# First norm of a hybrid encoder layer: TensorE turns x as it is loaded, the norm weights go on as a column behind the turn

## Chip, cores and metric

One core of a Trainium2 chip runs the whole layer as one program. The metric is device time in microseconds (us), median of the runs. Engines: PE is TensorE (PEld its weight loads), ACT is ScalarE, DVE is VectorE, POOL is GpSimd, SP is SyncE, which here only issues DMAs. 1 KB is 1024 bytes in the sizes of transfers.

## The reference, cut to what is computed

```
x = x + 1/2 * SwiGLU_1(RMSNorm(x, ffn1_norm))     # 2048 -> 2 x 5632 -> 2048
x = x + mix(RMSNorm(x, mix_norm))                 # dilated and differential attention, w_in, w_out
x = x + 1/2 * SwiGLU_2(RMSNorm(x, ffn2_norm))
rms_norm(x, g) = x * rsqrt(mean(x*x) + 1e-6) * g
swiglu_ffn(x) = (silu(gate) * up) @ w_out,  gate, up = split(rms_norm(x, g) @ w_in)
```

x is 256 rows of 2048 float32 values. Only the first norm, ahead of SwiGLU_1, is touched here.

## The kernel before

**Precision.** Every large product is made of three fp32r matmuls: an operand a is split into a_hi (rounded) and a_lo = a - a_hi, and hi·hi, hi·lo and lo·hi are added up in PSUM. So each piece of weights passes ACT (`split_hi`: w_hi is a rounded copy of w_raw) and then DVE (`split_lo`: w_lo = w_raw - w_hi) before TensorE may use it. Such a piece is a *unit*: two k-tiles of 128 by 512 columns, 128x1024 on chip, 12 matmuls of 512 columns. Units are numbered u0, u1, ... here. The ring of w_hi and w_lo has 4 places, so ACT may make unit u only when TensorE has used unit u-4. A weight load (`load`) brings 1024 KB, two units, into one of the 4 slots of w_raw. W0 is the load of u0 and u1, W1 that of u2 and u3, and so on; W4 is that of u8 and u9.

**The norm.** The factor rsqrt(...) of a row is applied later, to the product. What the matmuls need first is x·g, turned (transposed), in h_hi and h_lo. That is done in four chunks of 512 columns (four k-tiles each): SP loads a chunk of x and a chunk of the norm weights, the latter spread over all 128 partitions (`gain_row`); DVE multiplies them (`gain_x`, into `rows`); TensorE turns the product in 8 transposes (`turn_rows`, into `turn`); ACT copies it rounded to h_hi (`turn_split_hi`) and DVE subtracts to h_lo (`turn_split_lo`). Chunks 0 and 1 are turned before the first unit, chunk 2 between u0 and u1, chunk 3 between u3 and u4. The sum of squares of a row, for the factor, is made by ACT (`square_x`, two instructions for a chunk, each with an accumulator read).

**First stage of the FFN** (`hidden_first`): u0 to u7 make the first 512 columns of the gate, u8 to u15 those of the second half of w_in. u2 and u3 need chunk 1 of h, u4 and u5 chunk 2, u6 and u7 chunk 3. Each engine's order is written out by hand, and semaphores count units. Between the units DVE also makes the row factor (`norm_factor`, 14 tiny instructions in a chain, after `turn_split_lo` of chunk 3), `activation_wide` (after u9), `activation_sums` (after u10) and `split_sums` (after u11, waiting for ACT's s_hi), and only then w_lo of u12.

**The queue of SP** is one list: x and gain_row chunk by chunk with W0 to W2 between, then W3, then 17 small loads (rotary tables, head norm weights, lambda vectors; up to 64 KB each), then W4 on, each of these waiting for its slot.

The factor `splits` and the counters of `turn_hi` and `turn_split` number the turned chunks; `turn_rows(r, ...)` waits for `rows_ready` of r + 1.

Of the kernel before, what the change touches and what calls it, by code (L numbers as in the profile page):

```python
# [18 lines left out]
ALU = mybir.AluOpType  # L19
# [6 lines left out]
P = 128  # L26
# [93 lines left out]
IN1, OUT1, QKV, PROJ, IN2, OUT2 = range(6)  # L120
ROWS = np.cumsum([0, 4, FFN_ITERS, 4, 4, 4, FFN_ITERS]).tolist()
R_NORM1, R_FFN1, R_NORMX, R_MIX, R_NORM2, R_FFN2 = range(6)

# [30 lines left out]
def hybrid_layer_kernel(nc, x, ffn1_norm, ffn1_w_in, ffn1_w_out, mix_norm, w_in, a_q_norm, a_k_norm, b_q_norm,  # L156
# [8 lines left out]
    with ExitStack() as ctx:  # L165
# [24 lines left out]
        root = sb("root", [P, 88])  # L190
        gain_col = sb("gain_col", [P, 4])
        half_rstd = sb("half_rstd", [P, TT])

        with ExitStack() as hidden:
# [64 lines left out]

        x_landed = [sem(f"x_landed{c}") for c in range(4)]
        ident_landed = sem("ident_landed")
        const_landed = sem("const_landed")
        mask_landed = sem("mask_landed")
# [94 lines left out]
        def _(sp):  # L360
# [67 lines left out]

            gate_up1 = tiled(ffn1_w_in)  # L430
            for c in range(4):
                cols = slice(c * NC, (c + 1) * NC)
                sp.dma_start(x_sb[:, :, cols], x_dram[:, :, cols]).then_inc(x_landed[c], 16)
                sp.dma_start(gain_row[:, cols], ffn1_norm[:, cols].to_broadcast([P, NC])).then_inc(x_landed[c], 16)
                if c:
                    load(gate_up1, 0, KT * (c - 1), KT, c - 1)
            load(gate_up1, 0, KT * 3, KT, 3)
            sp.dma_start(cst[:, P:P + N_ROPE], consts[:, P + TT * SEQ:N_CONST]).then_inc(const_landed, 16)
            for gain, dst in ((a_q_norm, g_aq), (a_k_norm, g_ak), (a_out_norm, g_ao), (b_out_norm, g_bo),
                              (b_q_norm, g_bq), (b_k_norm, g_bk)):  # L440
# [12 lines left out]
            for g in range(GROUPS):  # L453
# [3 lines left out]
                if g == 0:  # L457
                    sp.wait_ge(units_used, UNIT[QKV])
                    sp.dma_start(mask[:, :, :], consts[:, P:P + TT * SEQ]
                                 .rearrange("p (t s) -> p t s", t=TT)).then_inc(mask_landed, 16)  # L460
            sp.wait_ge(rows_ready, ROWS[R_MIX])
            sp.dma_start(gain_row[:, :], ffn2_norm.to_broadcast([P, D])).then_inc(gain_landed, 16)
            proj_w = tiled(w_out)
            for n, (c, j) in enumerate(PROJ_ORDER):
# [10 lines left out]
        def _(pe):  # L475
# [27 lines left out]
            def turn_rows(r, buf, split, pair=None, copied=None):  # L503

                pair = buf if pair is None else pair
                pe.wait_ge(rows_ready, r + 1)
                if split is not None:
                    pe.wait_ge(turn_split, split)
                if copied is not None:
                    pe.wait_ge(turn_hi, copied)  # L510
                for k in range(4):
                    for t in range(TT):
                        mm = nc.tensor.transpose(turn4[pair][:, k, t * P:(t + 1) * P],  # L513
                                                 rows[:, buf, t, k * P:(k + 1) * P], ident)
                mm.then_inc(rows_turned, 1)

            h, act = (h_hi, h_lo), (act_hi, act_lo)

# [35 lines left out]
            def hidden_first(s_in, r0):  # L554

                u0 = UNIT[s_in]
                bank_wait(s_in, 0, 0)
                if s_in == IN1:
                    chunk(PARTS_D, u0, range(1), h, 0, r0 - 4)
                    turn_rows(r0 - 2, xg_at[2], splits(r0 - 3))  # L560
                    chunk(PARTS_D, u0, range(1, 4), h, 0, r0 - 4)
                else:
                    chunk(PARTS_D, u0, range(4), h, 0, r0 - 4)
                turn_rows(r0 - 1, 0, splits(r0 - 1))
                chunk(PARTS_D, u0, range(4, 8), h, 0, r0 - 4)
                bank_wait(s_in, 1, 0)
                chunk(PARTS_D, u0 + 8, range(8), h, 1)
# [171 lines left out]
            def attention_step(s):  # L739

                u, phase = divmod(s, 3)
                if phase == 0:
                    if u % HEADS_C == 2 and u > 2:
                        pe.wait_ge(turn_split, splits(ROWS[R_MIX] + u // HEADS_C))
                    if 1 <= u <= HEADS:
                        turn_weights(u - 1)
                    if u < HEADS:
                        turn_qk(u)
                if phase == 1:
                    if 1 <= u <= HEADS:  # L750
                        values(u - 1)
                    if u < HEADS:
                        scores(u)
                if turned_at(s):
                    g = u // HEADS_C - 1
                    pe.wait_ge(head_copied, u)
                    pe.wait_ge(rows_ready, ROWS[R_MIX] + g + 1)
                    for k in range(4):
                        for t in range(TT):
                            mm = nc.tensor.transpose(turn4[0][:, k, t * P:(t + 1) * P],  # L760
                                                     rows[:, g % 2, t, k * P:(k + 1) * P], ident)
                    mm.then_inc(rows_turned, 1)
# [13 lines left out]
                unit(UNIT[PROJ] + n, k0, count, (mix_hi, mix_lo), bank, (v == 0,) * TT, (v == UNITS_D - 1,) * TT)  # L776

            pe.wait_ge(ident_landed, 16)
            for c in range(2):
                turn_rows(ROWS[R_NORM1] + c, xg_at[c], None)  # L780
            ffn(IN1, OUT1, ROWS[R_FFN1], 0, False)
            for g in range(GROUPS):
                for j in range(SEG):
# [22 lines left out]
        def _(act):  # L806
# [43 lines left out]
            def turn_split_hi(r, dst, k, pair):  # L850
                act.wait_ge(rows_turned, r + 1)
                nc.scalar.activation(dst[:, bass.ds(k, 4), :], turn4[pair], ACT.Copy).then_inc(turn_hi, 1)

            def square_x(n, c):

                for t in range(TT):
                    before = 2 * (4 * n + c) + t
                    if before:
                        act.wait_ge(x_squared, before)
                    nc.scalar.activation(dump[:, :], x_sb[:, t, c * NC:(c + 1) * NC],  # L860
                                         ACT.Square, accum_out=sumsq[:, t, c:c + 1]).then_inc(x_squared, 1)
# [55 lines left out]
            def ffn(s_in, s_out, r0, n, updated, final):  # L917
# [2 lines left out]
                updated()  # L920
                square_x(2 * n, 3)
                split_hi(s_in, 6, 8, PARTS_D)
                turn_split_hi(r0 - 1, h_hi, 12, 0)
                split_hi(s_in, 8, 12, PARTS_D)
                act.wait_ge(s_raw_ready, S_GROUPS * n + 1)
                nc.scalar.activation(s_hi[:, :, :, :], s_raw, ACT.Copy).then_inc(s_hi_ready, 1)
# [122 lines left out]
            def copy_head(u):  # L1049
# [2 lines left out]
                act.wait_ge(head_done, u + 1)  # L1052
                if n == 0:
                    act.wait_ge(rows_turned, ROWS[R_MIX] + max(g - 1, 0))
                    act.wait_ge(rows_ready, ROWS[R_MIX] + g)
                if u:
                    act.wait_ge(head_copied, u)
                for t in range(TT):
# [11 lines left out]
            def attention_step(s, between=None):  # L1070
# [13 lines left out]
                if turned_at(s):  # L1084
                    g = u // HEADS_C - 1
                    turn_split_hi(ROWS[R_MIX] + g, mix_hi, 4 * g, 0)

            act.dma_start(cst[:, 0:P], consts[:, 0:P]).then_inc(ident_landed, 16)
            for c in range(2):
                turn_split_hi(ROWS[R_NORM1] + c, h_hi, 4 * c, xg_at[c])  # L1090
                split_hi(IN1, c, c + 1, PARTS_D)
            for c in range(2):
                act.wait_ge(x_landed[c], 32)
                square_x(0, c)
            split_hi(IN1, 2, 3, PARTS_D)
            turn_split_hi(ROWS[R_NORM1] + 2, h_hi, 8, xg_at[2])
            split_hi(IN1, 3, 4, PARTS_D)
            act.wait_ge(x_landed[2], 32)
            square_x(0, 2)
            ffn(IN1, OUT1, ROWS[R_FFN1], 0, lambda: act.wait_ge(x_landed[3], 32), False)  # L1100
            for g in range(GROUPS):
                for j in range(SEG):
                    if j % 4 == 0 and 3 * g + j // 4 > 0:
# [33 lines left out]
        def _(dve):  # L1137
# [43 lines left out]
            def turn_split_lo(r, dst_hi, dst_lo, k, pair):  # L1181
                dve.wait_ge(turn_hi, r + 1)
                nc.vector.tensor_tensor(dst_lo[:, bass.ds(k, 4), :], turn4[pair],
                                        dst_hi[:, bass.ds(k, 4), :].bitcast(F32),
                                        ALU.subtract).then_inc(turn_split, 1)

            def inverse_root(y, src, width, done=None, count=0):

# [108 lines left out]
            def out_sums(n, g):  # L1297

                if g:
                    dve.wait_ge(s_ready, S_GROUPS * n + 1 + g)  # L1300
                else:
                    dve.wait_ge(rows_ready, ROWS[R_FFN2 if n else R_FFN1] + FFN_ITERS)
                k0 = KT * S_BLOCKS[g]
                activation_sums(s_out_raw, *(act_raw[:, k0 + UK * half:k0 + UK * (half + 1), t * P:(t + 1) * P]
                                             for half in range(2) for t in range(TT)))
# [25 lines left out]
            def ffn(s_in, s_out, r0, n, final):  # L1331

                split_lo(s_in, 4, 8, PARTS_D)
                turn_split_lo(r0 - 1, h_hi, h_lo, 12, 0)
                norm_factor(2 * n)
                split_lo(s_in, 8, 10, PARTS_D)
                blocks = activation_wide()
# [245 lines left out]
                g = s // 3 // HEADS_C - 1  # L1583
                turn_split_lo(ROWS[R_MIX] + g, mix_hi, mix_lo, 4 * g, 0)

            for c in range(2):
                dve.wait_ge(x_landed[c], 32)
                gain_x(ROWS[R_NORM1] + c, c, 0)
            for c in range(3):
                if c == 2:  # L1590
                    split_lo(IN1, 2, 3, PARTS_D)
                turn_split_lo(ROWS[R_NORM1] + c, h_hi, h_lo, 4 * c, xg_at[c])
                if c:
                    dve.wait_ge(x_landed[c + 1], 32)
                    gain_x(ROWS[R_NORM1] + c + 1, c + 1, c)
                if c < 2:
                    split_lo(IN1, c, c + 1, PARTS_D)
            split_lo(IN1, 3, 4, PARTS_D)
            ffn(IN1, OUT1, ROWS[R_FFN1], 0, False)
            for g in range(GROUPS):  # L1600
                for j in range(SEG):
# [101 lines left out]
```

## Time and profile before

| | us |
|---|---|
| median of 3 runs | 1816.18 |
| lowest and highest | 1816.17, 1816.58 |
| profiled execution, its own time | 1815.82 |
| its span, first to last instruction | 1814.0 |
| TensorE busy in the span | 1798.8 |
| VectorE busy | 1533.5 |
| ScalarE busy | 1061.4 |

The span begins at 0 and all times of rows are counted from there. An instruction's row has its start and its duration; instructions of a kind in a row are merged (x8), and the duration is then from the start of the first to the end of the last. Square brackets give the time that the engine had been idle before it and what released it.

### The profile page before, as it was taken

How to read it: one execution, taken by the hardware profiler on the slowest of the kernel's cores; microseconds unless marked ns; L12 is line 12 of the kernel's file. 1: busy time of each engine (PE TensorE's matmuls, PEld its weight loads, DVE VectorE, ACT ScalarE, POOL GpSimd, SP SyncE). 2: the span in 40 equal slices, each digit the busy share in tenths (PEclk: the TensorE clock that was granted, in tenths of full speed). 3: DMA queues.
4: the chain of work that ended last, by engine and by line, in shares of the span. 5: the costliest groups of instructions: out<-in, count | busy, mean ns of one | idle time of the engine just before them, and what ended most of it. 6: DMA issues, size and time to landing. Idle time of an engine off the chain costs nothing.

```text
span 1814.0 us, 22680 instructions
## 1 busy us (share of the span) xinstructions
PE 1798.8 (99%) x8216; PEld 1492.7 (82%) x8216; DVE 1533.5 (85%) x1576; ACT 1061.4 (59%) x1273; POOL 43.1 (2%) x71
## 2 busy tenths in 40 slices
PE   7999999999999999999999999999999999999998
PEld 6888888888888888888888888888888888888887
DVE  6899999999999776667666666799999999989875
ACT  4666666666655555556556655566666566666453
POOL 0000000000000000111010000000000000000000
PEclk9999999999999999999999999999999999999999
DMA  8756656555346556654555445755566656254644
GB/s 291 255 203 222 217 193 215 200 185 185 124 178 229 211 202 208 201 182 146 172 164 179 156 163 185 255 187 207 186 215 217 214 193 220 96 186 165 253 162 162
DMA packets 178772, 353.03 MB, mean 195 GB/s; under 512 B 7184, under 2 KB 7824, under 8 KB 178448
## 3 DMA queue, kind: packets, MB, share of 16 engines
q1 hardware_dynamic: 178560, 352.07, 55.6%
q8 instruction: 41, 0.67, 0.1%
q14 instruction: 27, 0.22, 0.0%
q10 hardware_dynamic: 144, 0.07, 0.0%
HBM read 350.01 MB, written 2.10 MB: 194 GB/s over the span
## 4 chain that ended last, share of the span: by engine, by line
PE 99%; DMA 1%; DVE 0%; SPq 0%; ACT 0%; issue 0%
PE acc L484 14%; PE acc L486 14%; PE acc L485 14%; PE acc L529 8%; PE acc L527 8%; PE acc L528 8%; PE turn L541 4%; PE turn L540 4%; PE turn L542 4%; PE acc L541 3%; PE acc L540 3%; PE acc L542 3%; PE turn L513 2%; PE turn L600 1%; PE turn L602 1%; PE turn L601 1%
## 5 line engine op out<-in xcount | busy, mean ns | idle before, releaser
L1153 DVE TENSOR_TENSOR w_lo<-w_raw,w_hi 128x1024 fp32r<-128x1024 f32 x168 | 206.3, 1238 | 138.0 <-ACT w_hi L817 137.6
L817 ACT ACTIVATE w_hi<-w_raw 128x1024 fp32r<-128x1024 f32 x168 | 177.3, 1059 | 201.5 <-PE acc L486 179.4
L834 ACT ACTIVATE w_hi<-b 128x1024 fp32r<-128x1024 f32 x200 | 212.6, 1063 | 119.3 <-PE acc L529 77.4
L848 ACT ACTIVATE w_hi<-w_raw 128x1024 fp32r<-128x1024 f32 x180 | 190.1, 1059 | 145.7 <-PE acc L486 118.2
L1174 DVE TENSOR_TENSOR w_lo<-w_raw,w_hi 128x1024 fp32r<-128x1024 f32 x180 | 218.1, 1223 | 54.5 <-ACT w_hi L848 50.2
L529 PE MATMUL acc<-w_hi,h_lo 128*128 128x512 f32 x640 | 249.0, 389 | 0.0
L527 PE MATMUL acc<-w_hi,h_hi 128*128 128x512 f32 x640 | 249.0, 389 | 0.0
L528 PE MATMUL acc<-w_lo,h_hi 128*128 128x512 f32 x640 | 249.0, 389 | 0.0
L1164 DVE TENSOR_TENSOR w_lo<-b,w_hi 128x1024 fp32r<-128x1024 f32 x200 | 236.5, 1219 | 0.0
L834 ACT ACTIVATE w_hi<-w_raw 128x1024 fp32r<-128x1024 f32 x160 | 169.5, 1061 | 91.7 <-PE acc L529 64.1
L1164 DVE TENSOR_TENSOR w_lo<-w_raw,w_hi 128x1024 fp32r<-128x1024 f32 x160 | 193.8, 1221 | 14.8 <-ACT w_hi L834 11.7
L484 PE MATMUL acc<-w_hi,h_hi 128*128 128x512 f32 x512 | 203.6, 398 | 1.8 <-DVE w_lo L1153 1.8
L485 PE MATMUL acc<-w_lo,h_hi 128*128 128x512 f32 x512 | 200.0, 391 | 0.0
L486 PE MATMUL acc<-w_hi,h_lo 128*128 128x512 f32 x512 | 200.0, 391 | 0.0
L484 PE MATMUL acc<-w_hi,act_hi 128*128 128x512 f32 x512 | 199.8, 390 | 0.0
L486 PE MATMUL acc<-w_hi,act_lo 128*128 128x512 f32 x512 | 199.2, 389 | 0.0
L485 PE MATMUL acc<-w_lo,act_hi 128*128 128x512 f32 x512 | 199.2, 389 | 0.0
L834 ACT ACTIVATE w_hi<-t 128x1024 fp32r<-128x1024 f32 x80 | 85.0, 1062 | 103.7 <-PE acc L529 97.8
L529 PEld LDWEIGHTS acc<-w_hi,h_lo 128*128 128x128 f32 x640 | 120.2, 188 | 24.9
L527 PEld LDWEIGHTS acc<-w_hi,h_hi 128*128 128x128 f32 x640 | 120.2, 188 | 24.9
L528 PEld LDWEIGHTS acc<-w_lo,h_hi 128*128 128x128 f32 x640 | 120.2, 188 | 24.9
L484 PEld LDWEIGHTS acc<-w_hi,h_hi 128*128 128x128 f32 x512 | 96.6, 189 | 24.1 <-issue 4.8
(190 smaller groups left out, 3180.0 us busy)
## 6 DMA issues: line engine op xcount, KB each, us to landing
w_raw<-in_ffn_w_in SPq DMA_DIRECT2D x96, 1024.0 KB, 5.1
w_raw<-in_ffn_w_out SPq DMA_DIRECT2D x88, 1024.0 KB, 5.0
b<-in_ffn_w_in SPq DMA_DIRECT2D x80, 1024.0 KB, 5.0
w_raw<-in_w_in SPq DMA_DIRECT2D x48, 1024.0 KB, 5.1
w_raw<-in_w_out SPq DMA_DIRECT2D x16, 1024.0 KB, 5.0
x_sb<-in_x SPq DMA_DIRECT2D x4, 512.0 KB, 7.6
out_y<-x_sb SPq DMA_DIRECT2D x4, 512.0 KB, 5.1
gain_row<-in_ffn_norm SPq DMA_DIRECT2D x4, 256.0 KB, 8.1
```

What stands on the lines that cost most here:

```text
L484: nc.tensor.matmul(o, hi, w_hi[:, slot, kk, :], start=first[t] and kk == 0, stop=False)
L485: nc.tensor.matmul(o, hi, w_lo[:, slot, kk, :], start=False, stop=False)
L486: mm = nc.tensor.matmul(o, lo, w_hi[:, slot, kk, :], start=False, stop=last[t] and kk == count - 1)
L527: nc.tensor.matmul(o, hi, w_hi[:, slot, kk, :], start=kk == 0 and not begun, stop=False)
L528: nc.tensor.matmul(o, hi, w_lo[:, slot, kk, :], start=False, stop=False)
L529: mm = nc.tensor.matmul(o, lo, w_hi[:, slot, kk, :], start=False, stop=stop and kk == UK - 1)
L817: nc.scalar.activation(w_hi[:, u % RING, 0:count, :], w_raw[:, slot, k0:k0 + count, :], ACT.Copy).then_inc(hi_ready, 1)
L834: nc.scalar.activation(w_hi[:, slot, :, :], in_raw(piece)[:, k0:k0 + UK, :], ACT.Copy).then_inc(hi_ready, 1)
L848: nc.scalar.activation(w_hi[:, u % RING, :, :], src, ACT.Copy).then_inc(hi_ready, 1)
L1153: nc.vector.tensor_tensor(w_lo[:, slot, 0:count, :], w_raw[:, v // 2 % RAW, k0:k0 + count, :], w_hi[:, slot, 0:count, :].bitcast(F32), ALU ...
L1164: nc.vector.tensor_tensor(w_lo[:, slot, :, :], in_raw(piece)[:, k0:k0 + UK, :], w_hi[:, slot, :, :].bitcast(F32), ALU.subtract).then_inc(l ...
L1174: nc.vector.tensor_tensor(w_lo[:, u % RING, :, :], src, w_hi[:, u % RING, :, :].bitcast(F32), ALU.subtract).then_inc(lo_ready, 1)
```

## The change

- SP no longer loads gain_row for the first norm (four loads of 256 KB). ACT loads the norm weights as 16 rows of 128 values (`norm_in`, 8 KB) ahead of the identity matrix.
- TensorE turns x itself (`turn_x`), and once turns norm_in into 128 partitions by 16 columns; ACT copies that to `norm_col`.
- ACT makes h_hi per k-tile, 128x256, as turn times the column (`scale_hi`), DVE h_lo per k-tile as turn times column minus h_hi (`scale_lo`): 16 instructions on each in place of 4 of 128x1024; the four `gain_x` are gone.
- The first chunk of x is loaded, turned and split in two halves of 256 columns, and W0 in two halves of 512 KB, one per unit.
- Chunk 1 is turned behind u0 (no longer ahead of it), chunk 2 behind u1, chunk 3 behind u3 as before.
- ACT's squares of chunks 0 to 2 stand behind scale_hi of chunk 2, ahead of u4's w_hi; those of chunks 0 and 1 stood ahead of u2's before.
- Counters of `rows_ready` start 4 lower (UNREADY); nothing else in the later stages is touched.

```diff
+            half = NC // 2
+            sp.dma_start(x_sb[:, :, 0:half], x_dram[:, :, 0:half]).then_inc(x_half_landed, 16)
+            sp.dma_start(x_sb[:, :, half:NC], x_dram[:, :, half:NC]).then_inc(x_landed[0], 16)
+            sp.dma_start(w_raw[:, 0, 0:UK, :], gate_up1[:, 0:UK, 0:NC]).then_inc(w_half_landed, 16)
+            sp.dma_start(w_raw[:, 0, UK:KT, :], gate_up1[:, UK:KT, 0:NC]).then_inc(raw_landed[0], 16)
-            for c in range(4):
+            for c in range(1, 4):
                 cols = slice(c * NC, (c + 1) * NC)
                 sp.dma_start(x_sb[:, :, cols], x_dram[:, :, cols]).then_inc(x_landed[c], 16)
-                sp.dma_start(gain_row[:, cols], ffn1_norm[:, cols].to_broadcast([P, NC])).then_inc(x_landed[c], 16)
-                if c:
-                    load(gate_up1, 0, KT * (c - 1), KT, c - 1)
-            load(gate_up1, 0, KT * 3, KT, 3)
+                load(gate_up1, 0, KT * c, KT, c)
...
 # TensorE
+            def turn_x(c, pair, ks):
+                for k in ks:
+                    for t in range(TT):
+                        at = c * NC + k * P
+                        mm = nc.tensor.transpose(turn4[pair][:, k, t * P:(t + 1) * P], x_sb[:, t, at:at + P], ident)
+                return mm
+            def turn_norm(c, split):
+                pe.wait_ge(x_landed[c], 16)
+                if split:
+                    pe.wait_ge(turn_split, split)
+                turn_x(c, xg_at[c], range(4)).then_inc(rows_turned, 1)
...
-                    chunk(PARTS_D, u0, range(1), h, 0, r0 - 4)
-                    turn_rows(r0 - 2, xg_at[2], splits(r0 - 3))
-                    chunk(PARTS_D, u0, range(1, 4), h, 0, r0 - 4)
+                    pe.wait_ge(half_split, 1)
+                    chunk(PARTS_D, u0, range(1), h, 0)
+                    pe.wait_ge(norm_ready, 1)
+                    turn_norm(1, 0)
+                    pe.wait_ge(turn_split, 1)
+                    chunk(PARTS_D, u0, range(1, 2), h, 0)
+                    turn_norm(2, 1)
+                    chunk(PARTS_D, u0, range(2, 4), h, 0, r0 - 4)
+                    turn_norm(3, 2)
...
+            pe.wait_ge(x_half_landed, 16)
+            turn_x(0, xg_at[0], range(2)).then_inc(half_turned, 1)
+            pe.wait_ge(norm_landed, 16)
+            nc.tensor.transpose(turn[0][:, 0:KD], norm_in[:, :], ident[0:KD, 0:KD]).then_inc(norm_turned, 1)
+            pe.wait_ge(x_landed[0], 16)
+            turn_x(0, xg_at[0], range(2, 4)).then_inc(rows_turned, 1)
...
 # ScalarE
+            def scale_hi(c, ks, done):
+                for k in ks:
+                    s = nc.scalar.activation(h_hi[:, 4 * c + k, :], turn4[xg_at[c]][:, k, :], ACT.Copy,
+                                             scale=norm_col[:, 4 * c + k:4 * c + k + 1])
+                s.then_inc(done, 1)
...
+            act.dma_start(norm_in[:, :], ffn1_norm.rearrange("o (k p) -> (o k) p", p=P)).then_inc(norm_landed, 16)
             act.dma_start(cst[:, 0:P], consts[:, 0:P]).then_inc(ident_landed, 16)
+            act.wait_ge(norm_turned, 1)
+            nc.scalar.activation(norm_col[:, :], turn[0][:, 0:KD], ACT.Copy).then_inc(norm_ready, 1)
+            act.wait_ge(norm_ready, 1)
+            act.wait_ge(half_turned, 1)
+            scale_hi(0, range(2), half_hi)
+            act.wait_ge(w_half_landed, 16)
+            nc.scalar.activation(w_hi[:, 0, :, :], w_raw[:, 0, 0:UK, :], ACT.Copy).then_inc(hi_ready, 1)
+            act.wait_ge(rows_turned, 1)
+            scale_hi(0, range(2, 4), turn_hi)
+            split_hi(IN1, 1, 2, PARTS_D)
+            scale_norm(1)
+            split_hi(IN1, 2, 4, PARTS_D)
+            scale_norm(2)
+            act.wait_ge(x_half_landed, 16)
+            for c in range(3):
+                act.wait_ge(x_landed[c], 16)
                 square_x(0, c)
...
 # VectorE
+            def scale_lo(c, ks, done):
+                for k in ks:
+                    at = 4 * c + k
+                    s = nc.vector.scalar_tensor_tensor(h_lo[:, at, :], turn4[xg_at[c]][:, k, :], norm_col[:, at:at + 1],
+                                                       h_hi[:, at, :].bitcast(F32), ALU.mult, ALU.subtract)
+                s.then_inc(done, 1)
...
+            dve.wait_ge(norm_ready, 1)
+            dve.wait_ge(half_hi, 1)
+            scale_lo(0, range(2), half_split)
+            split_lo(IN1, 0, 1, PARTS_D)
+            dve.wait_ge(turn_hi, 1)
+            scale_lo(0, range(2, 4), turn_split)
+            split_lo(IN1, 1, 2, PARTS_D)
+            scale_norm(1)
+            split_lo(IN1, 2, 4, PARTS_D)
+            scale_norm(2)
```

## Rows read from the trace of the kernel before

**Rows 1.** The page, part 1: busy time, share of the span, instructions.

```profile
PE 1798.8 (99%) x8216; PEld 1492.7 (82%) x8216; DVE 1533.5 (85%) x1576; ACT 1061.4 (59%) x1273; POOL 43.1 (2%) x71
```

**Rows 2.** Waits of TensorE in the whole span: us, times, longest.

```profile
PE turn L513 <- DVE rows L1218: 8.9, 2, 8.0
PE acc L484 <- DVE w_lo L1153: 1.8, 1, 1.8
```

**Rows 3.** The chain that ended last: start, us, what.

```profile
2.75 9.35 DMA w_raw<-in_ffn_w_in
...
14.58 0.76 PE acc L484
...
16.20 0.43 PE acc L484
...
18.53 0.23 PE acc L484
...
19.23 0.87 PE turn L513 x8
...
29.16 0.23 PE acc L484
...
50.93 0.26 PE acc L484
```

**Rows 4.** First DMA issues, each alone: size, us from issue to landing.

```profile
x_sb<-in_x SPq DMA_DIRECT2D x1, 512.0 KB, 4.7
cst<-in_consts ACTq DMA_DIRECT2D x1, 64.0 KB, 3.5
...
gain_row<-in_ffn_norm SPq DMA_DIRECT2D x1, 256.0 KB, 5.3
```

**Rows 5.** Timeline of SP's queue: start and us of issues.

```profile
0.76 0.45 SPq L433 DMA_DIRECT2D x_sb<-in_x  x1
...
17.67 2.15 SPq L441 DMA_DIRECT2D gains<-in_b_q_norm  x1
...
26.18 4.91 SPq L365 DMA_DIRECT2D w_raw<-in_ffn_w_in  x4
```

**Rows 6.** Windows: stretch, busy us per engine, granted clock, DMA share, GB/s.

```profile
10.00:15.00 5.00, 2.39 (x9) 2.02 (x10) 3.76 (x4) 3.87 (x5) 0.00 (x0) 1.00 1.05 406
```

**Rows 7.** Timeline of TensorE: the first chunk's turn.

```profile
7.99 1.94 PE L513 MATMUL turn<-cst,rows 128*128 128x128 f32 x8 [7.99 <-DVE rows L1218]
```

**Rows 8.** Timeline of ScalarE in the first 40 us.

```profile
12.12 1.06 ACT L817 ACTIVATE w_hi<-w_raw 128x1024 fp32r<-128x1024 f32 x1 [1.14 <-DMA w_raw<-in_ffn_w_in]
...
14.93 0.62 ACT L860 ACTIVATE dump<-x_sb 128x512 bf16<-128x512 f32 x1
...
17.88 1.04 ACT L817 ACTIVATE w_hi<-w_raw 128x1024 fp32r<-128x1024 f32 x1
...
23.38 2.00 ACT L817 ACTIVATE w_hi<-w_raw 128x1024 fp32r<-128x1024 f32 x2
...
35.58 2.01 ACT L817 ACTIVATE w_hi<-w_raw 128x1024 fp32r<-128x1024 f32 x2 [5.22 <-DMA w_raw<-in_ffn_w_in]
```

**Rows 9.** Timeline of VectorE in the first 51 us.

```profile
13.21 1.23 DVE L1153 TENSOR_TENSOR w_lo<-w_raw,w_hi 128x1024 fp32r<-128x1024 f32 x1 [0.96 <-ACT w_hi L817]
...
31.75 0.15 DVE L1208 TENSOR_REDUCE rstd<-sumsq 128x2 f32<-128x8 f32 x1
...
34.31 0.17 DVE L1211 TENSOR_SCALAR half_rstd<-rstd 128x2 f32<-128x2 f32 x1
36.74 2.36 DVE L1153 TENSOR_TENSOR w_lo<-w_raw,w_hi 128x1024 fp32r<-128x1024 f32 x2 [2.27 <-ACT w_hi L817]
...
49.41 1.22 DVE L1153 TENSOR_TENSOR w_lo<-w_raw,w_hi 128x1024 fp32r<-128x1024 f32 x1
```

**Rows 10.** Timeline in the attention stage: nearest instructions to scale_hi and scale_lo.

```profile
786.51 0.82 ACT L1025 ACTIVATE qk_t<-turn,gain_col 128x256 f32<-128x256 f32 x2
...
799.53 0.88 DVE L1545 SCALAR_TENSOR_TENSOR weights<-probs,row_inv,masked 128x256 f32<-128x256 f32 x2
```

More of the change, by code:

```diff
@@ L122 @@
 R_NORM1, R_FFN1, R_NORMX, R_MIX, R_NORM2, R_FFN2 = range(6)
+UNREADY = 4
 TAIL = (0, 1, 1, 1, 1, 1, 2, 1, 1, 1, 1, 1, 1, 1, 2)
@@ L192, in hybrid_layer_kernel @@
         half_rstd = sb("half_rstd", [P, TT])
+        norm_col = sb("norm_col", [P, KD])
+        norm_in = sb("norm_in", [KD, P])
         with ExitStack() as hidden:
@@ L262, in hybrid_layer_kernel @@
         x_landed = [sem(f"x_landed{c}") for c in range(4)]
+        x_half_landed = sem("x_half_landed")
+        w_half_landed = sem("w_half_landed")
+        norm_landed = sem("norm_landed")
+        norm_turned = sem("norm_turned")
+        norm_ready = sem("norm_ready")
+        half_turned = sem("half_turned")
+        half_hi = sem("half_hi")
+        half_split = sem("half_split")
         ident_landed = sem("ident_landed")
@@ L460, in _ @@
                                  .rearrange("p (t s) -> p t s", t=TT)).then_inc(mask_landed, 16)
-            sp.wait_ge(rows_ready, ROWS[R_MIX])
+            sp.wait_ge(rows_ready, ROWS[R_MIX] - UNREADY)
             sp.dma_start(gain_row[:, :], ffn2_norm.to_broadcast([P, D])).then_inc(gain_landed, 16)
@@ L505, in turn_rows @@
                 pair = buf if pair is None else pair
-                pe.wait_ge(rows_ready, r + 1)
+                pe.wait_ge(rows_ready, r + (1 - UNREADY))
                 if split is not None:
@@ L558, in hidden_first @@
                 if s_in == IN1:
-                    chunk(PARTS_D, u0, range(1), h, 0, r0 - 4)
-                    turn_rows(r0 - 2, xg_at[2], splits(r0 - 3))
-                    chunk(PARTS_D, u0, range(1, 4), h, 0, r0 - 4)
+                    pe.wait_ge(half_split, 1)
[7 more added lines that the diff above has]
+                    turn_norm(3, 2)
                 else:
                     chunk(PARTS_D, u0, range(4), h, 0, r0 - 4)
-                turn_rows(r0 - 1, 0, splits(r0 - 1))
+                    turn_rows(r0 - 1, 0, splits(r0 - 1))
                 chunk(PARTS_D, u0, range(4, 8), h, 0, r0 - 4)
@@ L756, in attention_step @@
                     pe.wait_ge(head_copied, u)
-                    pe.wait_ge(rows_ready, ROWS[R_MIX] + g + 1)
+                    pe.wait_ge(rows_ready, ROWS[R_MIX] + g + 1 - UNREADY)
                     for k in range(4):
@@ L778, in _ @@
             pe.wait_ge(ident_landed, 16)
-            for c in range(2):
-                turn_rows(ROWS[R_NORM1] + c, xg_at[c], None)
+            pe.wait_ge(x_half_landed, 16)
[4 more added lines that the diff above has]
+            turn_x(0, xg_at[0], range(2, 4)).then_inc(rows_turned, 1)
             ffn(IN1, OUT1, ROWS[R_FFN1], 0, False)
@@ L852, in turn_split_hi, with scale_norm @@
                 nc.scalar.activation(dst[:, bass.ds(k, 4), :], turn4[pair], ACT.Copy).then_inc(turn_hi, 1)
+            def scale_hi(c, ks, done):
[3 more added lines that the diff above has]
+                s.then_inc(done, 1)
+            def scale_norm(c):
+                act.wait_ge(rows_turned, c + 1)
+                scale_hi(c, range(4), turn_hi)
             def square_x(n, c):
@@ L922, in ffn @@
                 split_hi(s_in, 6, 8, PARTS_D)
-                turn_split_hi(r0 - 1, h_hi, 12, 0)
+                if n == 0:
+                    scale_norm(3)
+                else:
+                    turn_split_hi(r0 - 1, h_hi, 12, 0)
                 split_hi(s_in, 8, 12, PARTS_D)
@@ L1054, in copy_head @@
                     act.wait_ge(rows_turned, ROWS[R_MIX] + max(g - 1, 0))
-                    act.wait_ge(rows_ready, ROWS[R_MIX] + g)
+                    act.wait_ge(rows_ready, ROWS[R_MIX] + g - UNREADY)
                 if u:
@@ L1086, in attention_step @@
                     turn_split_hi(ROWS[R_MIX] + g, mix_hi, 4 * g, 0)
+            act.dma_start(norm_in[:, :], ffn1_norm.rearrange("o (k p) -> (o k) p", p=P)).then_inc(norm_landed, 16)
             act.dma_start(cst[:, 0:P], consts[:, 0:P]).then_inc(ident_landed, 16)
[L1089 to L1093, printed above, removed]
-                square_x(0, c)
[L1095 to L1100, printed above, removed]
+            act.wait_ge(norm_turned, 1)
[14 more added lines that the diff above has]
+                act.wait_ge(x_landed[c], 16)
+                square_x(0, c)
+            ffn(IN1, OUT1, ROWS[R_FFN1], 0, lambda: act.wait_ge(x_landed[3], 16), False)
             for g in range(GROUPS):
@@ L1185, in turn_split_lo, with scale_norm @@
                                         ALU.subtract).then_inc(turn_split, 1)
+            def scale_lo(c, ks, done):
[4 more added lines that the diff above has]
+                s.then_inc(done, 1)
+            def scale_norm(c):
+                dve.wait_ge(turn_hi, c + 1)
+                scale_lo(c, range(4), turn_split)
             def inverse_root(y, src, width, done=None, count=0):
@@ L1301, in out_sums @@
                 else:
-                    dve.wait_ge(rows_ready, ROWS[R_FFN2 if n else R_FFN1] + FFN_ITERS)
+                    dve.wait_ge(rows_ready, ROWS[R_FFN2 if n else R_FFN1] + FFN_ITERS - UNREADY)
                 k0 = KT * S_BLOCKS[g]
@@ L1333, in ffn @@
                 split_lo(s_in, 4, 8, PARTS_D)
-                turn_split_lo(r0 - 1, h_hi, h_lo, 12, 0)
+                if n == 0:
+                    scale_norm(3)
+                else:
+                    turn_split_lo(r0 - 1, h_hi, h_lo, 12, 0)
                 norm_factor(2 * n)
@@ L1584, in turn_mixed @@
                 turn_split_lo(ROWS[R_MIX] + g, mix_hi, mix_lo, 4 * g, 0)
[L1586 to L1598, printed above, removed]
+            dve.wait_ge(norm_ready, 1)
[8 more added lines that the diff above has]
+            scale_norm(2)
             ffn(IN1, OUT1, ROWS[R_FFN1], 0, False)
```

## Prediction

> **What bounds the kernel now.** I read four views, in this order. The page says that TensorE is busy 1798.8 of 1814.0 us [rows 1]. The waits of TensorE over the whole span are only two: 8.9 us for the rows that DVE makes for the first turns, 1.8 us for the first w_lo [rows 2]. So all that any edit at the start can win lies before 14.58 us, where the first matmul begins [rows 3]; from there to the end TensorE is never seen waiting. The chain shows what set 14.58: load W0, issued at 2.75 and landed at 12.1, then w_hi 1.06 us on ACT and w_lo 1.23 us on DVE [rows 3, 8, 9]. It is the queue of transfers that sets the start, not the turns: by the order of the queue 2.5 MB of x, norm weights and W0 (a MB here is 1024 KB) come first.
>
> The chain also gives TensorE's own pace. A matmul takes 0.43 us at first and 0.23 us by 18.5 us [rows 3]. The granted clock reads 1.00 all along [rows 6], but 512 columns in 0.427 us is 1.2 GHz, and the later pace is near 2.4 GHz. Eight units last from 29.16 to 50.93, so 2.72 us each; eight transposes 0.87 us at that pace and 1.94 us at the lower one [rows 3, 7].
>
> The last view is the timeline of ACT and DVE past the start, since they must deliver each unit in time. There the slack is thin at one place: DVE ends w_lo of u12 at 49.41 + 1.22 = 50.63, and TensorE comes to u12 at 50.93 [rows 3, 9]. That chain on DVE starts with w_lo of u8 at 36.74, which waited for load W4 through ACT's w_hi at 35.58 [rows 8, 9].
>
> **The change, part by part.**
>
> *Transfers.* Removed are 4 x 256 KB ahead of the weights; ahead of u0's half of W0 stand 512 KB of x, so it is complete at 1.0 MB in place of 2.5. In full flow the DMAs move 406 GB/s, 2.6 us per MB [rows 6]. The first load of 512 KB is there at 0.76 + 4.7 = 5.5 us, the 768 KB with the first gain_row at about 1.26 + 5.3 = 6.6 (its issue follows the first one's) [rows 4, 5], W0, the 2.5th MB, at 12.1. Between the last two that is 3.15 us per MB, so 1.0 MB is there at 7.4, at full rate from 5.5 on at 6.8; I take 7.1. Halves cost packets of 1 KB in place of 2 KB for x, which no row prices; bound nothing to the whole of one more such load, 1.3 us. The first half of x, half the bytes of a load that took 4.7 us, lands at about 4.6 (bounds: 64 KB took 3.5 us, so 4.3, and 5.5). The identity is now second in ACT's queue: 0.45 us later, 0.75 + 0.45 + 3.5 = 4.7 (its issue before stood level with SP's first; 0.45 us is that of an issue).
>
> *The way to u0.* Four half-pace transposes from 4.7, 0.24 us each, end near 5.9 with the pipeline's tail; the norm's turn 6.1; ACT's copy of 128x16 and its own wait about 0.4 us: 6.5. Two scale_hi: the nearest row is ACT's copy out of PSUM with a column as scale, 128x256, 0.82 us for two [rows 10]: 7.3. w_hi of u0 follows from 7.35 to 8.4, and scale_lo (0.88 us for two by [rows 10]) lies beside it. w_lo ends at 9.7, first matmul at 9.85, with the latency of before. Start gained: 14.58 - 9.85 = 4.7 us.
>
> *TensorE's own work.* One more turn of eight stands between matmuls, that of chunk 1: +0.87 us. Of the lower pace: u0 whole at it is 12 x 0.427 = 5.1 us, before it was 14.58 to 19.2, where the next turn begins, 4.6 us [rows 3]. So chunk 1 is turned at 9.85 + 4.6 + 0.87 = 15.3 at best and at 9.85 + 5.1 + 1.94 = 16.9 if the lower pace lasts through both. I take 15.8. If nothing else held TensorE, u6 would begin at 15.8 + 5 x 2.72 + 2 x 0.87 = 31.1, against 29.16 + 2 x 2.72 = 34.6 before.
>
> *ACT is what holds it.* Before, ACT did the squares of chunks 0 and 1 while TensorE was at u0 (14.93 to 17.88: four in 2.95 us, 0.74 each) [rows 8]. Now ACT stops after w_hi of u1 (about 10.3) and waits until chunk 1 is turned, at 15.8, with none of its squares done. From there its list up to scale_hi of chunk 3 is: scale_hi of chunks 1 and 2 with 8 instructions 0.36 us apart (0.82 less 0.46, half the pair and the overlap), 2.9; w_hi of u2 to u7, six, at 0.97 us apart (2.00 for two, less 1.06, rounded up), 5.8; eight squares at 0.74, 5.9; four scale_hi, 1.5. That is 16.1 us. Then DVE's four scale_lo of chunk 3: pair 0.88, spacing 0.41, so 1.7; semaphores 0.2. u6 has its h_lo at 15.8 + 18.0 = 33.8. u2 and u4 also wait on the way, about 1 us each, for w_lo behind scale_lo and behind the squares; these waits are contained in the 2.7 us between 31.1 and 33.8. Of 4.7 us gained at the start 0.8 are left at u6. Everything that a wait here delays is TensorE's own queue, and the ring frees later; nothing else hangs on it.
>
> As to the price of scale_hi, the row has 0.36 us between two. The Trainium skill, page "ScalarE: Activation LUTs", section "What ACT_TABLE_LOAD costs", gives 186 ns plus 0.833 ns per element plus 93 ns for a pointer operand, less 93 ns of overlap: 0.40 us. An estimate by that page puts u6 12 x 0.04 = 0.5 us later. The sum goes by the row, since it has the same form of instruction.
>
> *DVE behind it.* norm_factor follows chunk 3's scale_lo, 31.75 to 34.48, 2.73 us [rows 9]: done at 36.6. w_lo of u8 begins then, 0.1 us ahead of 36.74, if W4 is there. As to W4: the stream of loads ahead of it is 1 MB shorter, so SP, held back by a full queue (as in the 2.15 us issue at 17.67), passes on 2.6 us sooner and issues W4 at about 23.6 in place of 26.18 [rows 5]; landed about 33, not 35.5. From w_lo of u8 to that of u12 the DVE's list is unchanged, 50.63 - 36.74 = 13.9 us: u12 ready at 50.5, and TensorE at u12 at 33.8 + 6 x 2.72 = 50.1 or, waiting, at 50.6 to 50.7. Before: 50.93. What remains is 0.25 us.
>
> *Later stages.* They are the same instructions; semaphore counts shifted by UNREADY cost nothing. The four gain_x taken from DVE won nothing but what hung on the first two, the 8.9 us of waits of [rows 2], and these lie ahead of the first matmul, which is counted above.
>
> The sum against the profiled time: 1815.82 - 0.25 = 1815.6 us. The median of the runs is 0.36 higher, their spread 0.4, so I keep 1815.6 for the median too. A difference of 0.2%, 3.6 us, is about what a measurement of this kernel tells from none; I forecast no change within it.
>
> **Rivals.**
> - *The start gain holds.* ACT and DVE keep up, and only the extra turn is paid: -4.7 + 0.9, 1812.0 us. For it: both have idle time up to 12 us. Against: the list above, with eight squares behind the turn. It would need ACT 2.7 us shorter and DVE's chain to u12 too. Chance 0.06.
> - *W4 does not come sooner*, or later by a little: the small loads are slow in themselves and SP issues them one by one. Then w_lo of u8 stays at 36.74 and nothing is gained: 1815.8 to 1816.2. For it: from 17.67 + 2.15 to 26.18 SP issued 11 small loads, 0.58 us each [rows 5], a time that a shorter stream ahead of them need not shorten. Chance 0.17.
> - *The lower pace lasts through the turn of chunk 1.* Then that is at 16.9, the list of ACT starts 1.1 us later, u12 0.85 us later than before: 1816.7 us. The trace has the rise once, within 3.9 us of the first matmul, and cannot say how it would fall with a start at 9.85. The Trainium skill, "TensorE: Matmul & The Clock Gate", section "What's actually happening", says that the number of slow matmuls varies between runs of the same kernel; by it this case stands open. Chance 0.15.
> - *The small instructions do not overlap.* At 0.46 us (ACT) and 0.48 (DVE) each, 12 x 0.10 + 4 x 0.07 = 1.5 us more up to u6: 1817.1 us. Against: the pairs of [rows 10]. Chance 0.10.
> - *Slower beyond doubt: TensorE stays at the lower pace.* The waits ahead of u2, u4 and u6, about 1 us each, break up its work so that the pace does not rise before u6. Then u0 to u5 take 6 x 5.1 and three turns 3 x 1.94, 36.4 us from 9.85: 46.3 in place of 34.6, +11.7, 1827.5 us. It passes 0.2% once three more units than u0 run so: 3 x 2.4 less the 2.7 us of waits that they fill, plus 0.85, is 5.4. Against: before, the pace had risen 3.9 us into u0, and u0 and the turn behind it are again without a gap. Chance 0.03.
>
> **How the numbers follow.** The likeliest case has 0.49 and a range of its own from 1814.9 (turn at 15.3) to 1816.4. The range for 8 in 10 takes in the second, third and fourth rivals and part of the way to the first, for landing times that I bounded loosely: 1813.4 to 1817.6. Faster by over 0.2% (below 1812.5) is only the first rival, and that not whole: 0.05. Slower by over 0.2% (above 1819.8) is the last: 0.03. Same: 0.92.
>
> **What the changed kernel's profile would show.** First matmul at 9.3 to 10.5 us; ACT idle for 4 to 6 us from about 10.3 until the turn of chunk 1; waits of TensorE inside u1 to u6 that add up to 2 to 3.5 us, the last ahead of u6 at about 34 us; ACT's w_hi of u8 not released by the DMA; u12 within 0.7 us of 50.7; from there on no new wait. The prediction is wrong if ACT's list from the turn of chunk 1 to u6 is much shorter than 18 us, if TensorE does not wait there, or if a wait turns up in a stage behind u16.

## The result, and the profile after

The changed kernel takes 1838.09 us (median of 4, 1837.71 to 1838.92) against 1816.38 (1816.17 to 1817.58): ratio 1.0120, 95% interval 1.0108 to 1.0133, 21.7 us slower. I had forecast 1815.6 and no change, with 1817.6 as the top of the range; 1838.09 lies 20.5 us above it.

The page, part 1, of the changed kernel (answers to [rows 1]): TensorE is busy 23 us longer with the same matmuls (one small turn more).

```profile
PE 1822.0 (99%) x8217; PEld 1493.2 (81%) x8217; DVE 1532.8 (83%) x1584; ACT 1063.5 (58%) x1286; POOL 43.0 (2%) x71
```

Its waits of TensorE in the whole span (answer to [rows 2]): 10.6 us against 10.7.

```profile
PE turn L535 <- DMA cst<-in_consts: 5.9, 1, 5.9
PE acc L497 <- DVE w_lo L1213: 4.4, 3, 2.5
PE acc L497 <- DVE h_lo L1251: 0.3, 1, 0.3
```

Its chain at the start (answers to [rows 3]):

```profile
1.24 4.58 DMA cst<-in_consts
...
10.74 0.77 PE acc L497
...
16.20 1.14 PE turn L535 x8
...
24.76 0.73 ACT dump L910 x2
...
33.69 1.67 DVE h_lo L1251 x4
35.41 0.50 PE acc L497
...
52.04 0.45 PE acc L497
```

u0 starts at 10.74 (before 14.58), but u6 waits for the squares on ACT ("dump") and for h_lo, and u12 begins at 52.04, 1.1 us later than before. The spans differ by 1837.1 - 1814.0 = 23.1 us, so 22 us arise behind u12, where TensorE waits for nothing. One window of the down projection of the first FFN, first of the kernel before, then of the changed one (columns as in [rows 6]), shows it: in 60 us of unbroken work 260 matmuls begin, not 266.

```profile
500.00:560.00 60.00, 60.00 (x266) 49.72 (x265) 53.86 (x52) 36.92 (x38) 0.00 (x0) 1.00 0.53 191
```

```profile
500.00:560.00 60.00, 60.00 (x260) 48.52 (x259) 53.18 (x52) 35.97 (x37) 0.00 (x0) 1.00 0.46 161
```

The granted clock reads 1.00 in both. The page's groups of the changed kernel (busy us, mean ns of one) say which matmuls got longer. Each matmul has two operands: one is loaded into the array first (h, act, s or mix), the other streams through it (w_hi or w_lo). The means are 395 to 396 ns where act is loaded and 390 to 392 where h is, with the same w_hi and w_lo streaming; in the kernel before the groups of act have 389 to 390.

```profile
L497 PE MATMUL acc<-w_hi,act_hi 128*128 128x512 f32 x512 | 203.0, 396 | 0.0
L498 PE MATMUL acc<-w_lo,act_hi 128*128 128x512 f32 x512 | 202.5, 396 | 0.0
L499 PE MATMUL acc<-w_hi,act_lo 128*128 128x512 f32 x512 | 202.4, 395 | 0.0
L499 PE MATMUL acc<-w_hi,h_lo 128*128 128x512 f32 x512 | 200.5, 392 | 0.0
L498 PE MATMUL acc<-w_lo,h_hi 128*128 128x512 f32 x512 | 200.4, 391 | 0.0
```

### The profile page after: what moved, and what is told of

It is laid out like the page before. It is cut to its first block, busy times and chain, and to the rows that moved or that the text cites. A ratio compares the mean times of both kernels' runs of the same rounds, so it can differ in the third digit from the quotient of the medians.

```text
span 1837.1 us, 22705 instructions
## 1 busy us (share of the span) xinstructions
PE 1822.0 (99%) x8217; PEld 1493.2 (81%) x8217; DVE 1532.8 (83%) x1584; ACT 1063.5 (58%) x1286; POOL 43.0 (2%) x71
## 4 chain that ended last, share of the span: by engine, by line
PE 98%; ACT 1%; DMA 0%; DVE 0%; issue 0%; ACTq 0%
PE acc L497 14%; PE acc L499 14%; PE acc L498 14%; PE acc L555 8%; PE acc L556 8%; PE acc L557 8%; PE turn L568 4%; PE turn L570 4%; PE turn L569 4%; PE acc L568 3%; PE acc L570 3%; PE acc L569 3%; PE turn L526 1%; PE turn L635 1%; PE turn L636 1%; PE turn L634 1%
## 6 DMA issues: line engine op xcount, KB each, us to landing
x_sb<-in_x SPq DMA_DIRECT2D x3, 512.0 KB, 10.5
```

## Experiments

The theory of place: the 22 us come from those 576 bytes. The rival: from the new instructions and loads. A pad of 144 float32 values is 576 unused bytes in every partition. Twelve kernels were run; "before" beside a time is the kernel before on the same chip.

**1. Both halves of the theory: the change without the shift, the shift without the change.**

```diff
 a_aligned (from the changed kernel)
         norm_in = sb("norm_in", [KD, P])
+        pad = sb("pad", [P, 112])
 b_pad576 (from the kernel before; b_pad64 and b_pad512 with 16 and 128 in place of 144)
         half_rstd = sb("half_rstd", [P, TT])
+        pad = sb("pad", [P, 144])
```

> The changed kernel with 448 unused bytes per partition behind norm_in, so that act_hi and all that is laid out behind it stands 1024 bytes further than before the change, not 576. Place theory (the matmuls whose turned operand lies behind the new buffers run 233 and not 227 ns apart because these operands have left their multiple of 1024 bytes): all matmuls back at 227 ns, 1817.5 us, that is 1.1 us of late start over before. Rival, that the new instructions or loads slow the whole run: 1838 us as the changed kernel.

> The kernel before the change with nothing but 576 unused bytes per partition between half_rstd and act_hi: no instruction differs. Place theory: 22 us longer than before, about 1838 us, with the same matmuls at 233 ns. Rival (instructions, loads, order at the start): 1816.4 us.

> As the last, with 64 bytes in place of 576. If it is the rest over 128 bytes that counts: 1838 us. If the rest over a larger block counts in steps, another time between 1816 and 1838. Rival as above: 1816.4.

> As the last, with 512 bytes. If only the 64 bytes count: 1816.4 us. If the operands must stand at a multiple of 1024 bytes: about 1838 us or in between.

| kernel | us | before | ratio, 95% interval |
|---|---|---|---|
| a_aligned | 1815.34 (10 runs) | 1816.51 | 0.9995, 0.9985 to 1.0004 |
| b_pad576 | 1838.28 (4 runs) | 1816.51 | 1.0118, 1.0101 to 1.0135 |
| b_pad64 | 1837.53 (1 run) | 1816.51 | |
| b_pad512 | 1816.12 (1 run) | 1816.51 | |

The rival falls. Unused bytes alone make the kernel before as slow as the changed one, and 448 more of them give the changed one its 22 us back. The interval of a_aligned takes in 1: without the shift the change is, as forecast, not told from none. Groups of act in a_aligned:

```profile
L498 PE MATMUL acc<-w_hi,act_hi 128*128 128x512 f32 x512 | 199.7, 390 | 0.0
L499 PE MATMUL acc<-w_lo,act_hi 128*128 128x512 f32 x512 | 199.2, 389 | 0.0
```

**2. Which step of the layout, and which operand.** b_pad32, b_pad128 and b_pad256 are as b_pad576 with 32, 128 and 256 bytes.

```diff
 b_moving (from the kernel before)
+        pad = sb("pad", [P, 16])
         w_hi = sb("w_hi", [P, RING, UK, NC], F32R)
         w_lo = sb("w_lo", [P, RING, UK, NC], F32R)
+        pad_end = sb("pad_end", [P, 240])
 b_hshift: the same two lines around h_hi and h_lo
 b_all64: the first of them alone, ahead of h_hi
```

> The kernel before with 128 unused bytes per partition ahead of act_hi. 64 bytes cost 21 us and 512 nothing. If a multiple of 128 bytes is enough: 1816.4 us. If it takes a multiple of 256 or 512: about 1838 us or in between.

> As the last, with 32 bytes, the smallest step of the layout. If every rest over 64 or 128 bytes costs the same: 1837.5 us. If the cost grows with the rest: between 1816 and 1837.

> The kernel before with 64 unused bytes ahead of w_hi and 960 behind w_lo: only w_hi and w_lo, the operands that stream through TensorE, leave their multiple of 1024 bytes. If it is the operand that is loaded into the array (h, act, mix, sums) whose address counts: 1816.4 us. If an operand of either kind counts, about all 8000 matmuls pay 6.6 ns: up to 1869 us.

> The kernel before with 64 unused bytes ahead of h_hi and 960 behind h_lo: only these two leave their multiple of 1024 bytes, act, mix and sums stay. If the loaded operand's address counts, the roughly 3,900 matmuls that load h run 233 ns apart and the others 227: 3,900 x 6.6 ns = 26 us more, 1842 us. If something else behind the new buffers was the cause (attention's tiles, act_raw, the blocks of w): 1816.4 us.

> The kernel before with 256 unused bytes per partition ahead of act_hi. 32, 64, 128 and 576 bytes cost 19 to 22 us, 512 nothing. If a multiple of 512 bytes is wanted: about 1835 us; if 256 is enough: 1816.4 us.

> The kernel before with 64 unused bytes ahead of h_hi and nothing behind: h, w_raw, w_hi, w_lo, act, mix and the sums other than s_lo all stand 64 bytes further, the same to each other as before. If the distance between the two operands of a matmul counted (both streams meeting in the same place): 1816.4 us. If the place of each operand by itself counts: at least the 31 us of h shifted alone, 1847 us or more, up to 1816 + 31 + 21 + 16 = 1884 us if the three shifts add up.

One run of each, with a profile. From the records of TensorE in each trace I took the time between the starts of neighbouring matmuls (those of 215 to 260 ns, some 7,500) and its mean by the operand that is loaded for the second one; ns:

```
loaded, number  before  changed  pad32  pad64  pad128  pad256  moving  hshift  all64
h_lo    1485    226.9   227.6    227.0  227.6  226.8   226.9   227.4   233.4   226.8
h_hi    2868    226.9   227.4    227.7  227.4  227.2   226.9   229.8   233.1   227.0
act_lo   584    226.8   233.4    233.2  233.4  232.6   226.5   227.6   227.2   226.5
act_hi  1156    226.7   233.2    233.3  233.2  232.5   226.8   229.6   227.2   226.8
s_hi     640    226.7   234.6    232.3  234.5  233.9   226.6   230.0   229.2   231.4
s_lo     320    226.6   229.1    230.5  229.2  233.9   226.7   226.7   227.9   230.6
mix_hi   226    227.8   233.3    233.2  233.3  232.5   227.9   230.5   227.7   228.3
mix_lo   128    227.6   233.3    233.0  233.3  232.0   227.4   226.9   227.4   227.1
time, us        1816.4  1838.1   1837.5 1837.5 1835.2  1816.9  1832.1  1846.9  1821.8
```

- 32, 64 and 128 bytes cost 19 to 22 us. 256 and 512 cost nothing: the one run of b_pad256 is 1.4 us above the run of the kernel before beside it (1815.43), but inside that kernel's own spread on the chip (1815.4 to 1817.3), and its matmuls keep their 227 ns. So what counts is the rest over 256, that is, the remainder of an address divided by 256; of the two answers weighed for b_pad256 the second came.
- The shift need not be act's. With h shifted alone, h pays 6.2 to 6.5 ns (b_hshift, 31 us against 1815.8, more than the 26 expected: these are 4,353 matmuls, not 3,900, and s pays 2 us too). With the streaming operand shifted alone there are 16 us to pay (b_moving); so my first wording, that only the loaded operand's address counts, was wrong. The guess of up to 1869 us for an operand of either kind was wrong as well: the three matmuls of one k-tile (hi·hi, hi·lo, lo·hi) start 680 ns apart in all in the kernel before, 700 where h or act stands 64 bytes off, but only 687 in b_moving (226, 229 and 232).
- b_all64 shows that it is a relation. h, w, act and mix all stand 64 bytes off a multiple of 256, and run at 227 ns as before. Only s pays, whose s_lo did not move with the others: (231.4 - 226.7) x 640 + (230.6 - 226.6) x 320 = 4.3 us of its 5.4 to 6.3. It is not the place of an operand by itself that counts. Where all loaded operands have the rest of the streaming one, nothing is paid.
- Which single matmul pays is not told by its own two operands. s_lo has the rest of w in b_pad64 and pays 2.6 ns; s_hi has it in b_all64 and pays 4.7. The records of b_hshift, where neither s nor w moved, show one reason: the 60 groups of s right behind h begin with eight starts that are 228 to 234 ns apart in the mean and go on at 226.7, while the 20 groups of s behind s have 226.7 from the first. A slow stretch reaches a few matmuls into the next operand's.
- Another rival is that TensorE's reads meet those of other engines, or DMAs. In b_pad64 the three matmuls of act take 700 ns where ACT, DVE and POOL are idle all the while (10 cases) and 700 where one of them is always busy (296); 700 without a DMA packet under way (131) and 700 with one always (331). So neither is needed for the cost.

The groups of b_all64 and b_hshift, in this order, show the same in the page's means:

```profile
L485 PE MATMUL acc<-w_hi,act_hi 128*128 128x512 f32 x512 | 199.7, 390 | 0.0
...
L543 PE MATMUL turn<-w_hi,s_lo 128*128 128x512 f32 x240 | 94.9, 395 | 0.0
```

```profile
L529 PE MATMUL acc<-w_hi,h_hi 128*128 128x512 f32 x640 | 253.1, 395 | 0.0
...
L486 PE MATMUL acc<-w_hi,act_hi 128*128 128x512 f32 x512 | 199.7, 390 | 0.0
```

**3. The start, with the pace restored.** The prediction named ACT's list as what eats the gain. In a_aligned ACT still stands idle for 5.1 us ahead of the turn of chunk 1 (its timeline):

```profile
9.04 1.07 ACT L856 ACTIVATE w_hi<-w_raw 128x1024 fp32r<-128x1024 f32 x1
15.20 1.57 ACT L896 ACTIVATE h_hi<-turn,norm_col 128x256 fp32r<-128x256 f32 x4 [5.08 <-PE turn L536]
```

```diff
 a_squares (from a_aligned)
             split_hi(IN1, 1, 2, PARTS_D)
+            act.wait_ge(x_half_landed, 16)
+            for c in range(3):
+                act.wait_ge(x_landed[c], 16)
+                square_x(0, c)
             scale_norm(1)
             split_hi(IN1, 2, 4, PARTS_D)
             scale_norm(2)
-            (the same four lines)
 a_squares_ident: ACT's loads of the identity and of norm_in exchanged as well
```

> The changed kernel with 448 unused bytes behind norm_in, and ACT's six squares of chunks 0 to 2 moved from behind scale_hi of chunk 2 to ahead of scale_hi of chunk 1, where ACT stood idle for 5.8 us in the aligned run. If ACT's list is what holds u4 and u6 (waits of 1.8 and 1.3 us or so, next to 0.9 us at u2): u4 and u6 are no longer waited for, and the end is 2 to 3 us sooner than the aligned kernel's 1815.3, at 1812.3 to 1813.3. Rival, that DVE's chain up to u12 or load W4 decides whatever ACT does: 1815.3 us.

> As a_squares, with ACT's two loads exchanged: the identity first, the norm weights second. The first turn waited for the identity until 5.9 us in the changed kernel and 5.1 in the aligned one. Identity landed at 4.3: u0 starts 0.5 to 0.8 us sooner, if not the first half of W0 holds it then, and the end comes 0 to 0.8 us sooner than a_squares.

| kernel | us | before | ratio, 95% interval |
|---|---|---|---|
| a_squares | 1813.87 (11 runs) | 1816.16 | 0.9987, 0.9978 to 0.9996 |
| a_squares_ident | 1813.83 (11 runs) | 1816.16 | 0.9985, 0.9976 to 0.9995 |

Waits of TensorE in a_aligned, then in a_squares. The second lost those of u4 and u6; of the 3.3 us left, 2.4 lie ahead of u0 and 0.9 ahead of u2.

```profile
PE turn L536 <- DMA cst<-in_consts: 5.1, 1, 5.1
PE acc L498 <- DVE w_lo L1214: 4.3, 3, 2.4
PE acc L498 <- DVE h_lo L1252: 0.3, 1, 0.3
```

```profile
PE turn L536 <- DMA cst<-in_consts: 5.8, 1, 5.8
PE acc L498 <- DVE w_lo L1214: 3.3, 2, 2.4
```

Both beat the kernel before by 2.3 us, by an interval that leaves out 1 though it reaches close to it. Against a_aligned it is 1.5 us by the medians, and 1.1 us when each is taken against the kernel before on its own chip (2.3 less 1.2), less than the 2 to 3 that I expected. The expectation had misread the trace of a_aligned: ACT is idle there for 5.1 us, not 5.8, and u4 and u6 wait 0.96 and 0.3 us, not 1.8 and 1.3. The chain of a_squares shows what is left:

```profile
10.52 0.76 PE acc L498
...
15.55 0.26 PE acc L500
15.81 0.89 PE turn L536 x8
...
27.85 0.23 PE acc L498
```

u0 starts 4.1 us sooner than before, u4 (27.85) only 1.3 us sooner than before (29.16); the turn of chunk 1, the wait ahead of u2 and a longer stretch at the lower pace, 5.0 us in place of 3.7, take the difference.

Exchanging the loads gains nothing measurable: with the identity early, the first half of x and then that of W0 are waited for instead. In the chain of a_squares_ident, issue to landing of that half is 5.94 us, and u0 starts at 10.21:

```profile
1.78 5.94 DMA w_raw<-in_ffn_w_in
7.75 1.07 ACT w_hi L1150
8.84 1.24 DVE w_lo L1214
10.21 0.77 PE acc L498
```

## Why the prediction was wrong

The step that failed is "Later stages. They are the same instructions; semaphore counts shifted by UNREADY cost nothing." The list of the change says the same: "nothing else in the later stages is touched". The instructions are the same; their operands are not in the same place. That term, put at nothing, measured 22 us: 6 to 8 ns on each matmul whose loaded operand moved by 576 bytes, without a new wait. By the table, excess over before by loaded operand in the changed kernel: act 11.4 us, s 5.9, h 2.6, mix 2.0, together 21.8 of the 22 us behind u12 (each the number of matmuls times the rise of their mean). The allocation of two buffers was nowhere in my sum, and the slow rival to which I gave 0.03, a lower clock held through u5, is not what happened: the pace rose within the turn behind u0. Nor would the signs that I listed have caught it: no wait turned up behind u16, and what grew was TensorE's busy time.

The rest of the sum, which a_aligned tests by itself, held within about 0.7 us at each step. Its chain, and the table:

```profile
1.24 3.79 DMA cst<-in_consts
...
9.84 0.77 PE acc L498
...
14.28 0.87 PE turn L536 x8
...
31.55 1.67 DVE h_lo L1252 x4
33.27 0.50 PE acc L498
...
49.92 0.41 PE acc L498
```

| step | forecast | changed | aligned |
|---|---|---|---|
| identity landed | 4.7 | 5.8 | 5.1 |
| first half of W0 landed | 7.1 | 8.3 | 7.0 |
| first matmul | 9.85 | 10.74 | 9.84 |
| chunk 1 turned | 15.8 | 17.3 | 15.2 |
| from there, ACT's list | 16.1 | 16.3 | 16.4 |
| u6 | 33.8 | 35.4 | 33.3 |
| W4 issued, landed | 23.6, 33 | 22.9, 32.5 | |
| u12 | 50.6 | 52.0 | 49.9 |
| time | 1815.6 | 1838.09 | 1815.34 |

That 1815.34 lies so near to 1815.6 is in part luck: u12 begins 1.0 us sooner than before, not 0.25, and the time is 1.2 us below that of the kernel before on its chip; that was 1816.51, 0.7 above the 1815.82 from which the sum started. In the changed kernel three signs fell just outside: first matmul 10.74 (9.3 to 10.5), ACT idle 6.4 us (4 to 6), u12 at 52.04 (50.0 to 51.4), behind loads that landed 1.1 to 1.2 us later than forecast and a lower pace that lasted through u0.

- *Transfers*: sized rightly for one execution, but they vary: 0.7 us in the identity, 1.3 in W0's half between two kernels with the same loads.
- *TensorE's own work*: the lower pace lasted through u0 and the start of the turn in the changed kernel (eight transposes in 1.14 us, between 0.87 and 1.94) and 3.3 us in the aligned one. My 15.8 lay between the 17.3 and the 15.2. Part of the third rival came true: in the changed kernel all of u0 ran at the lower pace.
- *ACT is what holds it*: right in place and size. u2, u4 and u6 waited as foretold, in the changed kernel 0.97, 0.89 and 0.3 us by its waits; a_squares shows by taking the squares away from the list that this was the cause.
- *The price of scale_hi*: four in 1.57 us, start to end, against 1.54 by the row and an estimate of 1.69 by the Trainium skill's page "ScalarE: Activation LUTs" ("What ACT_TABLE_LOAD costs"); the row was the better guide.
- *DVE behind it*: w_lo of u8 started at 38.0 in the changed kernel, right behind norm_factor, and no longer waited for W4, as said:

```profile
37.83 0.17 DVE L1284 TENSOR_SCALAR half_rstd<-rstd 128x2 f32<-128x2 f32 x1
38.03 2.36 DVE L1213 TENSOR_TENSOR w_lo<-w_raw,w_hi 128x1024 fp32r<-128x1024 f32 x2
```

- *The rivals* of a late W4 and of small instructions without overlap are excluded by these rows.

## What to carry to other kernels

Before you call a stage untouched, compare where its operands lie: a buffer of 64 bytes allocated in the middle can cost more than the edit can win. Put small buffers behind the large ones, or fill up to 256 bytes, and compare the count of matmuls in a window deep inside an unchanged stage before you explain anything at the edit. When the work of a start is rearranged, look for the idle time of the engine that becomes the limit: here six squares fitted into 5 us of it.

## What the runs showed of the hardware

In this kernel a matmul of 512 columns in fp32r starts 226.7 ns after the one before it when the loaded and the streaming operand have the same rest over 256 bytes in their partition, and about 233.3 ns, 6.6 more, where h alone or act alone stands 64 bytes off. Which of the reads collide is open. The cost is not symmetrical: three matmuls in a row pay 20 ns with h or act shifted by 64 bytes, 7 with the streaming operand shifted by 64. It also reaches into the next matmuls: eight of s behind h in b_hshift. s, whose two parts lie apart, pays between 2.6 and 7.9 ns with s_hi shifted by 64. Only shifts of 32, 64, 128, 256, 512, 576 and 1024 bytes were run, at this shape. Of the granted clock: in the kernel before, the trace's first record of it begins at 18.15 us, and the views print 1.00 for the time that has no record. Up to there 512 columns take 0.43 us, 1.2 GHz, and at 18.4 us they go over to 0.23 us; so the 1.00 of [rows 6] is no reading of the clock.
